# w_out split in heads 1 to 4, its product three tiles behind, and another order of the last head's tiles

## What is computed

```python
u = rms_norm(h, norm1_g)
q, k, v = jnp.split(h @ w_in, 3, axis=-1)         # h is u here; q, k normed by head
mask = key_chunk[None, :] <= q_chunk[:, None]      # chunks of 64 rows, causal
p = jax.nn.softmax(jnp.where(mask, s, -jnp.inf), axis=-1)
pd = (p[:, :, 0] - lam * p[:, :, 1])               # two maps of 64 channels a head
o = rms_norm(jnp.einsum('bhqs,bshe->bqhe', pd, v), sub_g) * (1.0 - lambda_init)
h = h + o.reshape(B, S, H * A_V_DIM) @ w_out
u = rms_norm(h, norm2_g)
h = h + jnp.square(jax.nn.relu(u @ mlp_w1)) @ mlp_w2
```

## Time and profile before

| | us |
|---|---|
| median of 3 runs | 2809.66 |
| lowest, highest | 2807.44, 2811.34 |
| profiled execution | 2807.01 |
| its span in the profile | 2805.2 |

### The profile page before, as it was taken

One profiled execution on the slowest core, in us unless ns is written; L12 is line 12 of the kernel. 1 busy time (PEld: TensorE's weight loads), 2 busy tenths in 40 slices (PEclk: granted clock), 3 DMA queues, 4 the chain that ended last, 5 costly groups with the idle time before them and its releaser, 6 DMA issues.

```text
span 2805.2 us, 42849 instructions
## 1 busy us (share of the span) xinstructions
PE 2724.4 (97%) x14784; PEld 2373.0 (85%) x14784; DVE 1897.3 (68%) x2726; ACT 1500.1 (53%) x2987; POOL 1076.3 (38%) x956
## 2 busy tenths in 40 slices
PE   7999999999999999979999999999999999999999
PEld 7998989989898999967887788888888888888887
DVE  6777787777778787775776666555555555666655
ACT  5666666666666666664554444444444444344443
POOL 5633424243433424331000354444343444444443
PEclk9999999999999999989999999999999999999999
DMA  8742424243242423223455996666667976666663
GB/s 263 263 146 84 163 97 152 95 147 116 95 153 85 162 97 128 98 87 140 154 184 182 352 371 239 236 237 254 269 244 280 361 282 234 234 233 238 236 236 131
DMA packets 181808, 544.09 MB, mean 194 GB/s; under 512 B 14736, under 2 KB 88208, under 8 KB 136592
## 3 DMA queue, kind: packets, MB, share of 16 engines
q1 hardware_dynamic: 180016, 541.25, 52.9%
q10 hardware_dynamic: 1632, 0.79, 0.1%
HBM read 470.81 MB, written 71.17 MB: 193 GB/s over the span
## 4 chain that ended last, share of the span: by engine, by line
PE 82%; issue 7%; DVE 5%; ACT 3%; DMA 2%; POOL 1%; SPq 0%; ACTq 0%; POOLq 0%; DVEq 0%
PE banks L2163 21%; PE banks L2139 21%; PE banks L421 17%; PE banks L666 5%; PE banks L563 4%; PE banks L565 4%; PE banks L638 4%; PE banks L825 2%; PE banks L668 2%; PE banks L513 2%; DVE mx L582 1%; ACT p_all L605 1%; DMA u<-u_factors 1%; DVE p_all L627 1%; ACT pt_hi L647 1%
## 5 line engine op out<-in xcount | busy, mean ns | idle before, releaser
L2139 PE MATMUL banks<-u,w 128*128 128x512 f32 x2688 | 614.6, 390 | 3.6 <-issue 2.1
L421 PE MATMUL banks<-w_hi,u_ring 128*128 128x384 f32 x2048 | 590.4, 348 | 12.1 <-DVE u_ring L1315 4.0
L2139 PEld LDWEIGHTS banks<-u,w 128*128 128x128 f32 x2688 | 505.4, 188 | 109.8 <-issue 3.7
L2163 PE MATMUL banks<-w,a_hi 128*128 128x512 f32 x1792 | 551.9, 389 | 1.6 <-issue 1.1
L1905 POOL TENSOR_TENSOR w<-w_raw,w 128x1024 fp32r<-128x1024 f32 x96 | 245.2, 2568 | 553.2 <-ACT w L1954 278.2
L605 ACT ACTIVATE p_all<-banks,bias 128x1024 f32<-128x1024 f32 (+7 forms) x384 | 331.7, 866 | 182.9 <-DVE bias L585 116.3
L2163 PEld LDWEIGHTS banks<-w,a_hi 128*128 128x128 f32 x1792 | 336.3, 188 | 72.1 <-issue 2.4
L421 PEld LDWEIGHTS banks<-w_hi,u_ring 128*128 128x128 f32 x2048 | 376.5, 189 | 17.4 <-issue 11.4
L2163 PE MATMUL banks<-w,a_lo 128*128 128x512 f32 x896 | 348.6, 389 | 0.0
L451 POOL TENSOR_TENSOR qk_rs<-qk_var,minus_half 128x4 f32<-128x4 f32 x128 | 129.5, 1011 | 564.7 <-DVE qk_var L445 564.7
L421 PE MATMUL banks<-w_lo,u_ring 128*128 128x384 f32 x1024 | 344.9, 337 | 0.0
(11 more groups left out here) (151 smaller groups left out, 4730.1 us busy)
## 6 DMA issues: line engine op xcount, KB each, us to landing
u<-u_factors SPq DMA_DIRECT2D x224, 1024.0 KB, 9.4
u_ring<-u_scratch SPq DMA_DIRECT2D x112, 1024.0 KB, 5.2
w_raw<-in_mlp_w SPq DMA_DIRECT2D x128, 512.0 KB, 6.7
u_scratch<-u_ring SPq DMA_DIRECT2D x16, 1024.0 KB, 4.9
u_factors<-q_hi SPq DMA_DIRECT2D x23, 512.0 KB, 4.3
u_factors<-q_lo SPq DMA_DIRECT2D x23, 512.0 KB, 4.4
w_raw<-in_a_w_in SPq DMA_DIRECT2D x90, 128.0 KB, 4.6
p_all<-in_x SPq DMA_DIRECT2D x16, 512.0 KB, 5.7
```

What stands on the lines that cost most here:

```text
L421: last = pe.matmul(proj[:, 0:3 * HD], u[:, part, kt, :], w[:, kt, :], start=(kt == 0 and part == 0 and w is w_hi), stop=(kt == KT - 1 and ...
L2139: last = pe.matmul(banks[:, UP_BANKS[p] + f, :], w[:, 2 * k2 + k, f * P:(f + 1) * P], u[:, :, part, k, :], start=(STARTS[p] and k2 == 0 an ...
L2163: last = pe.matmul(banks[:, DOWN_BANKS[p] + t, :], a[:, p % 2, f, t * P:(t + 1) * P], b[:, f, :], start=(STARTS[p] and f == 0 and a is a_h ...
```

## The change

w_out is split in heads 1 to 4: piece kt (a row block of 128) at j = 2 and j = 5 of each. SP loads the raw piece one step before into the upper half of plane 0 of P, ACT writes the high part and DVE (not POOL) the low part into the upper halves of planes 1 and 2, and SP stores both to a new DRAM tensor at j = 3 and j = 6. At the end of head 6 and in steps 0 and 1 of head 7 both parts are loaded into their places at 0 and 32 KB. `OUT0` becomes 3: the first product is made at j = 3, and two stages of the loop stand behind the last head's own (14 and 15 behind 13). The last head takes its tiles in the order 4 to 7, 0 to 3, 8 to 15, and the output tiles follow that order; the counts of semaphores are summed along it. The last head's own columns of o are no longer loaded from DRAM in any tile: PE takes them from `o_sum`, once normed. The places of the factors change with the order, and the final store of the result puts its rows where they belong.

```diff
-OUT0 = 4
+OUT0 = 3
+W_OUT_HEADS = (1, 2, 3, 4)
+LAST_ORDER = (4, 5, 6, 7, 0, 1, 2, 3, 8, 9, 10, 11, 12, 13, 14, 15)
+def tile_of(a):
+    h, j = a // NT, a % NT
+    return LAST_ORDER[j] if h == H - 1 else j
...
+def split_w_out(h, j, first):
+    return 2 * (h - W_OUT_HEADS[0]) + (j - first) // 3 if h in W_OUT_HEADS and j in (first, first + 3) else None
...
+    w_out_raw = p_all[:, 0, D:2 * D]
+    w_out_split = p_stage[:, 1:3, D:2 * D]
...
     def dve_output(dve, a):
-        if a >= 2:
+        if a >= ALL - NT + 2:
+            dve.wait_ge(o_turned, 2 * ((a - 2) % NT) + 2)
+        elif a >= 2:
             dve.wait_ge(o_stored[par], 16 * (a // 2))
...
+    def load_raw_w_out(sp, kt):
+        if kt:
+            sp.wait_ge(w_out_lo_set, kt)
+        sp.dma_start(w_out_raw, w_out[kt * P:(kt + 1) * P, :]).then_inc(w_out_raw_loaded, 16)
     def high_w_out(act, kt):
+        act.wait_ge(w_out_raw_loaded, 16 * (kt + 1))
+        if kt:
+            act.wait_ge(w_out_stored, 32 * kt)
+        act.activation(w_out_split[:, 0, :], w_out_raw, ACT.Copy).then_inc(w_out_hi_set, 1)
     def low_w_out(engine, kt):
         engine.wait_ge(w_out_hi_set, kt + 1)
+        engine.tensor_tensor(w_out_split[:, 1, :], w_out_raw, w_out_split[:, 0, :].bitcast(F32), ALU.subtract)\
+            .then_inc(w_out_lo_set, 1)
+    def store_w_out(sp, kt):
+        sp.wait_ge(w_out_lo_set, kt + 1)
+        for part in range(2):
+            sp.dma_start(w_out_parts[part, kt], w_out_split[:, part, :].bitcast(F32)).then_inc(w_out_stored, 16)
...
     def load_o(sp, t):
+        tile = LAST_ORDER[t]
+        a = ALL - 2 * NT + tile
+        cols = slice(0, D - HD)
...
     def pe_turn_o(pe, t):
-                if t >= NT - 2 and kt == KT - 1:
+                if kt == KT - 1:
                     pe.wait_ge(o_normed, ALL - NT + t + 1)
                     rows = o_sum[:, t % 2, :]
...
     def sync(sp):
+            kt = split_w_out(h, j, 1)
+            if kt is not None:
+                if j == 1:
+                    sp.wait_ge(p_turned, groups_through(a - 2))
+                load_raw_w_out(sp, kt)
+            kt = split_w_out(h, j, 3)
+            if kt is not None:
+                store_w_out(sp, kt)
+            place = a - (ALL - NT - US + 1)
+            if 0 <= place < US:
+                if place == 0:
+                    sp.wait_ge(w_out_stored, 32 * KT)
+                sp.wait_ge(proj_half, 2 * (ALL - US + place + 1))
+                for kt in (2 * place, 2 * place + 1):
+                    load_w_out(sp, 0, kt)
             if h == H - 1 and j < 2:
                 for kt in range(j * HALF, (j + 1) * HALF):
+                    load_w_out(sp, 1, kt)
+            if h == H - 1 and j == 1:
+                load_o(sp, 0)
+                load_x(sp, 0)
...
     def gpsimd(pool):                       # small_step
-            if h == H - 1 and j <= 3:
-                low_w_out(pool, 2 * j)
-                low_w_out(pool, 2 * j + 1)
...
     def scalar(act):                        # small_step, behind act_square_output(act, a - 1)
+            kt = split_w_out(h, j, 2)
+            if kt is not None:
+                high_w_out(act, kt)
...
     def vector(dve):                        # small_step, behind dve_output(dve, a - 1)
+            kt = split_w_out(h, j, 2)
+            if kt is not None:
+                low_w_out(dve, kt)
```

More of the change, by code:

```diff
@@ L73, in own_mask, with sums_of, split_step @@
     return banks_of(t) <= 2
-def masks_through(a, m):
-    h, t = a // NT, a % NT
-    return 2 * (h * sum(own_mask(i) for i in range(NT)) + sum(own_mask(i) for i in range(t))) + m + 1
-GROUPS = sum(banks_of(t) for t in range(NT))
-PIECES = sum(count_of(t) for t in range(NT))
-WIDE = sum(count_of(t) for t in range(NT) if count_of(t) > 1)
+def sums_of(count):
+    sums = [0]
+    for a in range(H * NT):
+        sums.append(sums[-1] + count(tile_of(a)))
+    return sums
+GROUPS = sum(banks_of(t) for t in range(NT))
+MASKS_TO = sums_of(lambda t: int(own_mask(t)))
+GROUPS_TO = sums_of(banks_of)
+PIECES_TO = sums_of(count_of)
+WIDE_TO = sums_of(lambda t: count_of(t) if count_of(t) > 1 else 0)
+SUMS_TO = sums_of(lambda t: int(count_of(t) > 1))
+def masks_through(a, m):
+    return 2 * MASKS_TO[a] + m + 1
 def split(a):
     return a // NT, a % NT
+def split_step(a):
+    return a // NT, tile_of(a)
 def group_count(a, n):
-    h, t = split(a)
-    return h * GROUPS + sum(banks_of(i) for i in range(t)) + n + 1
+    return GROUPS_TO[a] + n + 1
 def groups_through(a):
-    return group_count(a, banks_of(a % NT) - 1)
+    return GROUPS_TO[a + 1]
 def piece_count(a, m, k):
-    h, t = split(a)
-    return 2 * (h * PIECES + sum(count_of(i) for i in range(t))) + m * count_of(t) + k + 1
+    return 2 * PIECES_TO[a] + m * count_of(tile_of(a)) + k + 1
 def scores_through(a):
-    return piece_count(a, 1, count_of(a % NT) - 1)
+    return 2 * PIECES_TO[a + 1]
 def wide_count(a, m, k):
-    h, t = split(a)
-    return 2 * (h * WIDE + sum(count_of(i) for i in range(t) if count_of(i) > 1)) + m * count_of(t) + k + 1
+    return 2 * WIDE_TO[a] + m * count_of(tile_of(a)) + k + 1
 def sums_through(a):
-    h, t = split(a)
-    return h * sum(count_of(i) > 1 for i in range(NT)) + sum(count_of(i) > 1 for i in range(t + 1))
+    return SUMS_TO[a + 1]
 def last_users():
@@ L126, in last_users @@
         for m in range(2):
-            for k, (first, banks, place) in enumerate(pieces_of(a % NT, m)):
+            for k, (first, banks, place) in enumerate(pieces_of(tile_of(a), m)):
                 users[a, m, k] = [held[b] for b in range(place, place + banks) if b in held]
@@ L147, in turn_order @@
         qk = [("qk", a + NT - 1)] if a + NT - 1 < H * NT else []
-        p = [("p", a - 1, n) for n in range(banks_of((a - 1) % NT))] if a else []
+        p = [("p", a - 1, n) for n in range(banks_of(tile_of(a - 1)))] if a else []
         t = output_tile(h, j)
@@ L545, in pe_scores @@
     def pe_scores(pe, a, m):
-        h, t = split(a)
+        h, t = split_step(a)
         if m == 0:
@@ L588, in act_exp @@
     def act_exp(act, a, m, k):
[L589 removed]
+        t, par = tile_of(a), a % 2
         if k == 0:
@@ L598, in act_exp @@
                 act.wait_ge(combined, a)
+            if m == 0 and t == BIG and a // NT in W_OUT_HEADS:
+                act.wait_ge(w_out_stored, 64 * (a // NT - W_OUT_HEADS[0] + 1))
             for tile, plane, place in ((BIG, 0, 8), (BIG, 1, 10), (BIG + 1, 0, 9)):
-                if a == ALL - NT + tile and m == plane:
+                if a == step_of(tile) and m == plane:
                     act.wait_ge(u2_stored[place], 16 * STAGED[place])
@@ L635, in pe_turn_p @@
         wait_slot(pe, "p", a, n)
-        for c in range(bank_width(a % NT, n) // P):
+        for c in range(bank_width(tile_of(a), n) // P):
             at = n * BANK + c * P
@@ L1377, in small_step @@
         def small_step(a, n, nb):
-            t = output_tile(*split(a))
+            h, j = split(a)
+            t = output_tile(h, j)
             dve_max(dve, a, 0, 0)
@@ L1833, in store_y @@
                 sp.wait_ge(y_added, ((c + 1) * NB - 1) * ADDS + 2 * LAST_ADDED[q] + half + 1)
-                sp.dma_start(quarter(1, c, q, tiles),
+                pair = LAST_ORDER[2 * (c * TPB + 2 * half)] // 2
+                out_tiles = slice(pair % TPB, pair % TPB + 2)
+                sp.dma_start(quarter(1, pair // TPB, q, out_tiles),
                              y[:, th * TPB + 2 * half:th * TPB + 2 * half + 2, dh * BANK:(dh + 1) * BANK])\
```

80 lines of the change are left out of this document (35 added, 45 removed).

## The result

The changed kernel takes 2827.5 us (median; 2822.9 to 2828.9) against 2807.9 for the kernel before on the same chip: ratio 1.0069, 95% interval 1.0058 to 1.0081, slower by some 19.6 us. The forecast was 2828.2: 18.5 us on a base of 2809.7, the median of the three runs known then, where six runs give 2807.9. Its profiled execution has 2827.2 (span 2825.1), which is 19.9 us more span than before. The total came out as forecast; its terms did not all, and that is what the rest is about.

A forecast was written before the change was run, and what follows sets the result against it. PE, busy 97% of the span, was taken as the bound, so only its idle and half-clock time could change. 12.2 - 8.8 + 11.4 - 2.8 + 6.5 = +18.5 us on 2809.7 gave 2828.2 us, range 2806 to 2838.

The forecast's parts named there:

- Part 1: Splits in heads 1 to 4: Vector 2.6 us late, PE waits 1.9 and 1.1 us a head, +12.2 us in all.
- No fall: Splits in heads 1 to 4: PE's clock stays whole after the 1.9 us wait at j = 2; 6.8 us kept for the range.
- rival (a): Heads 1 to 4: the clock falls after each wait at j = 2, adding 6.8 us, 2835 us; chance 0.13.
- Part 2: Last head's hole before the first product: product 4.5 us earlier and 4.3 us of work done ahead, -8.8 us.
- Parts 3 and 4: Last head's products: waits and half clock from the reorder, +11.4 us; end of the attention: shorter wait, clock kept, -2.8 us.
- five idle times: PE waits between products of the reordered small tiles, the last before tile 8: 10.2 us together, against 2.5 before.
- term of -1.2: Last head's products: shorter tiles remove some 1.2 us of short waits (first residual, slots of the normed rows).
- The MLP's start: First MLP product: weights and the transfers queued behind them move 7 us against PE, +6.5 us.
- Rival (b): First MLP product: the transfers of the first MLP tile hide, taking off 6.5 us, 2821.7 us; chance 0.08.
- (c): Heads 1 to 4 and MLP start: splits and first MLP transfers both hide, no change, 2809.5 us; chance 0.10.
- (e): Heads and products: small work never reaches PE, lags made up before PE asks, -23.3 us, 2804.9 us; chance 0.12.
- (d): Last head: the first product stays at about its old time, losing 4.5 us of gain, 2832.7 us; chance 0.04.

The follow-up runs named there:

- other three corners: The changed kernel with the old tile order (2822.7 us), with the product four tiles behind (2827.3 us), or with both (2817.8 us).
- e1: The changed kernel without the splits' eight Scalar copies and eight Vector subtractions in heads 1 to 4, all transfers kept: 2810.8 us.
- e2: The changed kernel with the eight subtractions of w_out on GpSimd instead of Vector, at the same place: 2810.6 us.
- e6: The changed kernel with the last head's old tile order and the product four tiles behind, so only the splits remain: 2817.8 us.
- e5: The changed kernel with the last head's tiles in the old order 0 to 15, product still three behind: 2822.7 us.
- e3: The changed kernel with Vector's split subtraction one step later and SP's store moved one step too: 2818.1 us.
- e4: The changed kernel with tile 13's store of h ahead of the first MLP weights and tile 15's load of x ahead of the u loads: 2822.5 us.
- e7: The changed kernel with GpSimd's subtraction (as e2) and SP's order at the end (as e4) together: 2805.2 us.

## Why the prediction was right

**The bound.** PE at 96% and the time moving with PE's idle and half-clock time: shown, the work in the two middle windows is 296.2 to 297.5 us in before, after and the other three corners, while their length goes from 331.0 to 341.4.

**Part 1, mechanism right, size short.** Predicted 12.2 (its own 4 x 3.0 is 12.0), measured 17.6 us (e1 and e2 give 16.7 and 16.9 back). Vector's lag was 2.65 (2.6 predicted), the wait at j = 2 1.83 (1.9). Three things were missing. At j = 5 PE waits 1.44, not 1.1: not ahead of the values but ahead of a transposition that stands before them in its queue, so the slack of the earlier trace rows was read at the wrong instruction. PE's timeline of the kernel before has it 0.35 us ahead of the values, with a slack of 1.2:

```profile
641.50 0.60 PE L513 MATMUL banks<-ident,qk_nat 128*128 128x128 f32 x4
```

0.3 us of the lag reaches step 8. And each head has 0.5 us more busy PE time, which waits alone don't show; its cause stays open. The clock was the fourth: of the five profiles with Vector's subtraction in steps 2 and 5 (20 heads) it fell in 8, after the same wait (1.83 or 1.84 us). Two such waits of 1.83 us of the changed kernel, by the windows that begin with them:

```profile
464.10:469.00 4.90, 4.87 (x32) 1.00 0.81 267
628.60:633.50 4.90, 4.82 (x22) 0.65 0.79 266
```

One at full clock, one at 0.65. "No fall", and rival (a), "always", were both too simple; 1.7 us for one head of four here.

**Part 2, too cautious.** Predicted 8.8, measured 11.3 us of lost time: the product comes 7.9 us earlier for 4.5, with 3.3 us more work done ahead of it for 4.3. The steps of tiles 5 and 6 were right (8.7 and 7.7 us for 8.3 and 8.0, from one tile's last values to the next's). The values of tile 15 ended 1.2 us sooner than I took, and from the end of the transposition to the product it took 2.1 us for 4.3, because the clock was whole again:

```profile
1276.55 1.72 PE L836 MATMUL banks<-ident,o_in 128*128 128x128 f32 x7
...
1278.85 0.39 PE L593 MATMUL banks<-k_s,q_hi 128*128 128x512 f32 x1
```

That the splits lengthened the hole is shown by e6: with the old order and distance it is 5.6 us shorter. Scalar's copies left together with GpSimd's subtractions (and the loads of w_out and of o are those of the change), so what GpSimd's part alone is worth stays open. Vector's combination of 256 columns, 2.46 us in the earlier trace rows, takes 0.48 in the last head of e5:

```profile
1267.31 0.48 DVE L659 SCALAR_TENSOR_TENSOR p_all<-p_all,neg_c 128x256 f32<-128x256 f32 x1
```

The Trainium skill (GPSIMD Engine Reference, Specifications) says that the two engines share their SBUF interfaces; the trace agrees (2.46 against 0.48 us). The collision of the new subtraction with GpSimd's small work did not come in the changed kernel, where it takes 1.23 us; it came in e3, where the subtraction grows to 1.69 us beside GpSimd.

The 25.0 us lost of 41.0, read off before the sum, were short: busy time was multiplied by a PEclk that is the mean over the whole stretch, idle time included. By busy time at half clock it is 26.9 of 40.7.

**Parts 3 and 4, long waits right, clock less.** Predicted +11.4 and -2.8, +8.6 together; measured +7.3, of which idle time is +7.6 (6.9 predicted) and half clock -0.3 (+1.7 predicted). The five idle times were forecast as 1.6, 1.8, 3.1, 1.1 and 2.6 and came as 1.45, 1.38, 2.96, 0.92 and 2.55, for instance:

```profile
1336.71 0.66 PE L670 MATMUL banks<-ident,p_all 128*128 128x128 f32 x2 [2.96 <-DVE ot_lo L851]
...
1372.02 0.50 PE L876 MATMUL banks<-w_out_hi,ot_hi 128*128 128x512 f32 x1 [2.55 <-DVE ot_lo L851]
...
1545.01 1.15 PE L670 MATMUL banks<-ident,p_all 128*128 128x128 f32 x7 [1.90 <-DVE q_hi L991]
```

The clock fell at the 2.96 and not at the 2.55; it fell also at 1319.5, behind the wait of 1.38. That there are two new stretches, as forecast, is luck: in the six profiles with this order three behind (this one, e1 to e4, e7) the waits are the same within 0.05 us, and the stretches under the products number 2, 4, 2, 2, 0 and 2. No term had a third change: before, the first product began in a stretch at half clock that lasted until 1275.1, 1.9 us of loss that is gone. The normed output of the tile before the last cost one wait of 1.06 us and short ones after it of 0.4 in all, near the 1.5. At the last tile the wait is 1.90 instead of 2.62, with the clock whole, where 1.1 was taken: the chain of sums no longer decides, and the sum of the part (2.8) was nearly reached by 0.7 of wait and the clock that isn't lost. The term of -1.2 failed: the short waits that the shorter tiles were to remove stayed, 1.77 us for Vector's first residual against 0.79 before, and 0.98 for the slot of the normed rows against 1.2.

**The MLP's start, right.** Predicted 6.5, measured 6.65 us, a wait of 6.55 us at the place named, x issued 20.5 us after the stage of tile 14 began (1557.97), and e4 takes 4 to 5 of it back by moving two entries of SP's queue. That the half clock behind the wait costs nothing more was wrong by 1.1 us. Rival (b) is out, and (a) came true in one head of four.

**So** the mechanisms were right, and the closeness of the sum is partly luck, two errors that cancel: 12.2 - 0.2 + 6.5 was forecast, 17.6 - 4.3 + 6.65 measured; the base of 2809.7 brought the total nearer still. Both misses lay within the bounds named for their terms (0 to 21, and -14 to -4 for the hole). Rivals (c) and (e) needed the splits to hide, which e1 refutes; (d) needed the product at its old time, and it starts 7.9 us sooner after the mark.

## What to carry to other kernels

Moved work is free only in an engine that nobody waits for at that place: the same subtraction cost 17 us in Vector's queue, in front of what PE takes next, and nothing in GpSimd's, where it takes twice as long. Price a moved instruction by its lag (the wait for its input included), and compare it with the slack at the first instruction of PE's queue that hangs on the late engine, not at the one you think of. And when a stage is brought forward, count lost time (idle and half clock), not distance between marks, and look at the end of the region for the transfers that had been hidden by the stage that is gone.

## What the hardware showed that I had not expected

- The clock after a wait doesn't follow from the wait's length: after 1.83 us it fell in 8 of 20 cases and stayed in 12; at the wait of 2.55 it fell in 2 of 6 profiles (e1, e3), at that of 2.96 in 4 of 6 (not in e4 and e7).
- PE's busy time grows by 0.5 us a head (157.36 to 157.82) with two waits in it at unchanged instructions and whole clock; why is not shown.
- A small instruction can lose most in a collision of Vector and GpSimd: in e3 GpSimd's 128 x 128 subtraction took 1.45 us instead of 0.46 beside Vector's of 1024 columns and ended at 628.17, 0.33 after it; Vector's took 1.69 instead of 1.23. Times on POOL are rough, and this is one place.
- A wait for a store can be a wait for the queue ahead of it: 15.8 us lie between the issue of a 512 KB store of h and that of the load that needs its buffer; in e4, where the store goes out ahead of the weights, it is 6.8 (1553.45 to 1560.21), with weights and factors issued in between.
